# A software pipeline over the heads of a delta rule, and a reordered convolution stage, in a six-layer flow-matching trunk

## What is computed

```
def conv_module(h, w1, b1, dw, dwb, lng, lnb, w2, b2, on_grid):
    a = h @ w1 + b1
    a = a[..., :D_MODEL] * jax.nn.sigmoid(a[..., D_MODEL:])
    a = (dwconv_grid(a, dw) if on_grid else dwconv_seq(a, dw)) + dwb
    a = jax.nn.silu(layer_norm(a, lng, lnb))
    return a @ w2 + b2

def delta_rule_chunked(q, k, v, log_a, beta, s0):
    ...
    a_mat = beta[..., :, None] * jnp.einsum("bhnid,bhnjd->bhnij", k, k) * dec_strict
    rhs = jnp.concatenate([beta[..., None] * v, (beta * jnp.exp(g))[..., None] * k], -1)
    sol = lax.linalg.triangular_solve(eye + a_mat, rhs, left_side=True, lower=True, unit_diagonal=True)
    u_t, w_t = sol[..., :dv], sol[..., dv:]
    p_mat = jnp.einsum("bhnid,bhnjd->bhnij", q, k) * dec_incl
    ...
    def step(s, inp):
        u = ut - jnp.einsum("bhck,bhkv->bhcv", wt, s)
        o = jnp.einsum("bhck,bhkv->bhcv", qt, s) + jnp.einsum("bhij,bhjv->bhiv", pt, u)
        s = gt[..., None, None] * s + jnp.einsum("bhck,bhcv->bhkv", kt, u)
        return s, o
```

## Time and profile before

| what | value |
| --- | --- |
| median of 3 runs | 1915.3 us (1914.95 to 1916.79) |
| the profiled execution, its own time | 1915.8 us |
| its span | 1914.0 us |
| PE busy | 1820.6 us (95%) |
| DVE, ACT, POOL busy | 997.1, 815.5, 266.5 us |
| mean granted TensorE clock | 0.984 of full speed |
| P of head 0 to the last output product of head 7 | 1360.4 to 1541.9 us |
| conv taps on PE | 435.8 to 486.4 us |

### The profile page before, as it was taken

How to read it: one execution, slowest core, us unless ns; L and a number is a source line. 1 busy time by engine, 2 the same in 40 slices (tenths; PEclk the granted TensorE clock), 3 DMA queues, 4 the chain that set the end, 5 groups by cost and what they waited for, 6 DMA issues and landing times.

```text
span 1914.0 us, 30887 instructions
## 1 busy us (share of the span) xinstructions
PE 1820.6 (95%) x11265; PEld 1677.1 (88%) x11265; DVE 997.1 (52%) x1684; ACT 815.5 (43%) x1334; POOL 266.5 (14%) x317
## 2 busy tenths in 40 slices
PE   5999999998999999999999999899899999999998
PEld 3899999688679999988999998878788867999997
DVE  3433444898473434455344448756555547444444
ACT  1333332777553444235444326454444435444322
POOL 2000000476420000010000003000222222000001
PEclk8999999999999999999999999999899989999999
DMA  9774344763566344456444445422000034444440
GB/s 325 219 220 126 117 137 148 255 231 88 186 202 205 112 131 122 134 174 186 131 131 117 134 145 147 131 56 67 9 11 11 11 102 121 127 118 128 133 129 35
DMA packets 369963, 254.16 MB, mean 133 GB/s; under 512 B 9715, under 2 KB 350307, under 8 KB 369891
## 3 DMA queue, kind: packets, MB, share of 16 engines
q1 hardware_dynamic: 369104, 252.89, 43.5%
q10 hardware_dynamic: 787, 0.32, 0.1%
HBM read 250.55 MB, written 2.62 MB: 132 GB/s over the span
## 4 chain that ended last, share of the span: by engine, by line
PE 83%; DVE 8%; issue 3%; DMA 2%; ACT 2%; SPq 1%; DVEq 0%; POOL 0%; ACTq 0%
PE bank L1512 23%; PE bank L1514 23%; PE bank L1513 23%; PE bank L1575 3%; DMA mod_raw<-in_w_mod 2%; PE bank L1940 1%; SPq L470 1%; PE bank L1783 1%; DVE w_lo L997 1%; PE bank L1539 1%; PE bank L1934 1%; PE bank L1751 1%; PE bank L1760 1%; PE bank L1627 1%; PE bank L1798 1%
## 5 line engine op out<-in xcount | busy, mean ns | idle before, releaser
L1512 PE MATMUL bank<-h_hi,w_hi 128*128 128x384 f32 x1920 | 655.5, 341 | 5.3 <-POOL h_lo L599 3.0
L1514 PE MATMUL bank<-h_hi,w_lo 128*128 128x384 f32 x1920 | 644.9, 336 | 0.0
L1513 PE MATMUL bank<-h_lo,w_hi 128*128 128x384 f32 x1920 | 644.6, 336 | 0.0
L997 DVE TENSOR_TENSOR w_lo<-w_raw,w_hi 128x1024 fp32r<-128x1024 f32 x336 | 434.3, 1314 | 190.6 <-ACT w_hi L724 188.3
L724 ACT ACTIVATE w_hi<-w_raw 128x1024 fp32r<-128x1024 f32 x336 | 344.4, 1050 | 313.4 <-PE bank L1514 294.4
L1512 PEld LDWEIGHTS bank<-h_hi,w_hi 128*128 128x128 f32 x1920 | 362.2, 189 | 39.3 <-issue 29.8
L1513 PEld LDWEIGHTS bank<-h_lo,w_hi 128*128 128x128 f32 x1920 | 362.4, 189 | 0.1
L1514 PEld LDWEIGHTS bank<-h_hi,w_lo 128*128 128x128 f32 x1920 | 362.1, 189 | 0.0
L1513 PE MATMUL bank<-act_lo,w_hi 128*128 128x384 f32 x704 | 236.1, 335 | 0.0
L1514 PE MATMUL bank<-act_hi,w_lo 128*128 128x384 f32 x704 | 236.0, 335 | 0.0
L1512 PE MATMUL bank<-act_hi,w_hi 128*128 128x384 f32 x704 | 236.0, 335 | 0.0
(11 more groups left out here) (307 smaller groups left out, 1795.1 us busy)
## 6 DMA issues: line engine op xcount, KB each, us to landing
w_raw<-in_ffn_w_in SPq DMA_DIRECT2D x176, 512.0 KB, 4.7
mod_raw<-in_w_mod SPq DMA_DIRECT2D x132, 512.0 KB, 5.3
w_raw<-in_ffn_w_out SPq DMA_DIRECT2D x64, 448.0 KB, 3.8
w_raw<-in_ffn_w_out SPq DMA_DIRECT2D x32, 512.0 KB, 4.0
w_raw<-in_dn_w_in SPq DMA_DIRECT2D x32, 512.0 KB, 4.0
w_raw<-in_cv_w SPq DMA_DIRECT2D x24, 512.0 KB, 4.3
mod_early<-in_w_mod SPq DMA_DIRECT2D x12, 512.0 KB, 10.0
w_raw<-in_dn_w_out SPq DMA_DIRECT2D x8, 512.0 KB, 4.1
```

Source lines behind the costliest of these rows:

```text
L997: dve.tensor_tensor(w_lo[:, slot], w_raw[:, slot], w_hi[:, slot].bitcast(F32), ALU.subtract).then_inc(w_lo_ready, 1)
L1512: pe.matmul(ps, w_hi[:, w_slot, k], a_hi, start=start, stop=False)
L1513: pe.matmul(ps, w_hi[:, w_slot, k], a_lo, start=False, stop=False)
L1514: return pe.matmul(ps, w_lo[:, w_slot, k], a_hi, start=False, stop=stop)
```

## The change

**Heads.** The loops go over pairs of heads with the buffers that must last doubled (`inv`, `inv_t`, scores, q_decay, k_head; the second set lies in the place of h_hi and h_lo, which are free there), and the last two heads stand behind the loop. Norm spreads, row spreads, scalings, gate differences, exponentials and k·k of head h + 1 are done inside head h, one after the other through bank 7; DVE makes the next head's matrix at the end of head h. Only q·k stays at the start of a head, ahead of P, in bank 7 too.
**Beta.** The system is solved with beta on the columns in place of the rows; so beta isn't spread any more (two of four row spreads go), POOL doesn't multiply v (one copy of the first tile is left, `v_first`), the matrix takes one DVE instruction per tile and direction, and ACT's copy of u has beta as its scale.
**Conv.** ACT makes a row product behind each diagonal, not behind each second; `store_taps` stands 18 diagonals later; PE turns the groups ahead of tap 31, not of tap 8. DVE's list is unchanged there.

```diff
@@ PE, heads
-                with pe.Fori(0, H) as h:
-                    pe.wait_ge(qk_ready, 2 * h + 2)
-                    pe.wait_ge(head_done, h + 1)
-                    for ps, m in ((bank[6], k_head), (bank[7], q_head)):
...
+                def spread_k_norm(n):
+                    pe.wait_ge(sel_ready, n + 1)
+                    spread(bank[7], sel_qk[:, 1], qk_rnorm_hi[:, :], qk_rnorm_lo[:, :]).then_inc(norm_spread, 1)
+                def spread_q_norm(n):
+                    pe.wait_ge(qk_ready, 2 * n + 1)
...
+                def spread_row(n, d):
+                    if d == 0:
+                        pe.wait_ge(qk_ready, 2 * n + 2)
+                    else:
+                        pe.wait_ge(q_exp_ready, 2 * n + 1)
+                    spread(bank[7], sel_row[:, d], rows_hi[:, :], rows_lo[:, :]).then_inc(rows_spread, 1)
...
+                def k_products(n, q):
+                    pe.wait_ge(q_exp_ready, 2 * n + 2)
+                    gram_of(k_heads[q], k_heads[q], kk_ready)
+                def head(h, p, more):
...
+                        if m == 0:
+                            pe.wait_ge(a_step, 2 * h + 2)
+                            gram_of(k_of, q_head, qk_product)
...
+                        if m == 1 and more:
+                            spread_q_norm(h + 1)
...
+                        if m == 0 and more:
+                            pe.wait_ge(scored, 2 * h + 2)
+                            spread_k_norm(h + 1)
...
+                        if m == 1 and more:
+                            spread_row(h + 1, 0)
...
                     solve(0, t_joined, (h + 1) * (2 * UPPER) - 1)
+                    if more:
+                        spread_row(h + 1, 1)
                     solve(1, x_set, 4 * h + 1)
...
-                    pe.wait_ge(sel_ready, h + 2)
-                    spread_norms()
+                    if more:
+                        k_products(h + 1, 1 - p)
+                    solve(2, x_set, 4 * h + 3)
@@ ACT, heads: exponentials(h + 1, 1 - p, 0) behind the levels, and
+                            act.activation(u_sb[:, k % 2, d], u_bank(k, d)[:, 0:P], ACT.Copy,
+                                           scale=beta[:, SCAN[d][k], ds(h + d * H, 1)]).then_inc(u_copied, 1)
                         if k == 1:
+                            if more:
+                                exponentials(h + 1, 1 - p, 1)
                             act.wait_ge(state_in, 16 * h + 16)
                             for d in range(2):
                                 act.wait_ge(s_added, 4 * h + d + 1)
                                 act.activation(s_out[:, d], bank[4 + d][:, 0:P], ACT.Copy).then_inc(s_stored, 1)
@@ DVE, heads
+                def matrix(n, q):
+                    dve.wait_ge(kk_ready, n + 1)
+                    for d in range(2):
+                        dve.wait_ge(decay_ready, 2 * n + d + 1)
+                        for t in range(NT):
+                            last = dve.scalar_tensor_tensor(decay[:, d, t], scores[q][:, d, t], minus_beta[:, t, ds(n + d * H, 1)],
+                                                            bank[7][:, t * P:(t + 1) * P], ALU.mult, ALU.mult)
+                        last.then_inc(a_step, 1)
@@ ACT, conv
+        STORE_LATER = DIAGS + 6
                         diagonal(n)
-                        if n % 2 and left:
+                        if left:
                             row_product(*left.pop(0))
                         for o in (PE_CHUNK, *PE_SEQ):
-                            if n == taps_used(o) + DIAGS - 12:
+                            if n == taps_used(o) + STORE_LATER:
                                 store_taps(o)
@@ PE, conv
                     for n, (o, tap) in enumerate(PE_TAPS):
-                        if n == 8:
+                        if n == TAPS:
                             turn_groups(mod_glu)
```

More of the change, by code:

```diff
@@ L849, in delta_on_scalar @@
                     act.activation(o_all[:, ds(h, 1)], bank[6][:, 0:T].unsqueeze(1), ACT.Copy).then_inc(head_done, 1)
+                for d in range(2):
+                    exponentials(0, 0, d)
+                with act.Fori(0, H // 2 - 1) as i:
+                    for p in range(2):
+                        head(2 * i + p, p, True)
+                for p in range(2):
+                    head(H - 2 + p, p, p == 0)
                 act.wait_ge(head_done, H + 1)
@@ L1335, in delta_on_vector, with head @@
+                        last.then_inc(a_step, 1)
+                def head(h, p, more, select_next):
+                    dve.wait_ge(qk_product, h + 1)
+                    for d in range(2):
+                        dve.tensor_tensor(scores[p][:, d], scores[p][:, d], tiles(bank[7]), ALU.mult).then_inc(scored, 1)
                     for n in range(BASE_LEVEL, LEVELS):
@@ L1364, in delta_on_vector @@
                                                          bank[4 + d][:, 0:P], ALU.mult, ALU.add).then_inc(s_updated, 1)
+                    if more:
+                        matrix(h + 1, 1 - p)
+                scale_k(0, 0)
+                scale_q(0)
+                for d in range(2):
+                    differences(0, 0, d)
+                select(1, 0)
+                matrix(0, 0)
+                with dve.Fori(0, H // 2 - 1) as i:
+                    for p in range(2):
+                        head(2 * i + p, p, True, True)
+                for p in range(2):
+                    head(H - 2 + p, p, p == 0, False)
                 dve.wait_ge(head_done, H + 1)
@@ new lines, in gram_of, with head @@
+                def gram_of(first, second, done):
+                    for t in range(NT):
+                        mm = pe.matmul(bank[7][:, t * P:(t + 1) * P], first[:, t * P:(t + 1) * P], second[:, t * P:(t + 1) * P], start=True, stop=True)
+                    mm.then_inc(done, 1)
+                def k_products(n, q):
+                    pe.wait_ge(q_exp_ready, 2 * n + 2)
+                    gram_of(k_heads[q], k_heads[q], kk_ready)
+                def head(h, p, more):
+                    k_of, inv_of, inv_t_of = k_heads[p], invs[p], invs_t[p]
```

198 lines of the change are left out of this document (102 added, 96 removed).

## The result

| | before | changed |
|---|---|---|
| median, us | 1915.3 (1914.21 to 1917.98, 5 runs) | **1906.1** (1903.84 to 1908.79, 5 runs) |
| ratio, 95% interval | 1 | **0.9948** (0.9935 to 0.9961) |
| profiled execution, its time | 1915.8 | 1908.8 |
| its span | 1914.0 | 1907.0 |
| mean granted clock | 0.984 | 0.984 |

The change makes the kernel faster by 0.52%, 9.2 us in the medians. The forecast was 1896, 19 us faster, with a range of 1888 to 1907: the sign was right and the time lies inside the range, near its upper end, but only half of the gain came; that the time is inside is owed to the width of the range. The profiled execution after is itself 2.7 us above its median, so by place I compare its span with that of before, 7.0 us less; between kernels the medians decide.

The account below looks back on a forecast made before the run. PE was taken to bound the kernel (83% of its chain of waits). Start of heads +6.1, seven periods -19.9, last head -1.0 and conv -4.9 sum to -19.7 us: 1896 by the median, range 1888 to 1907.

Parts of the forecast that it names:

- The start of the heads: Head 0's preparation runs one step after another through bank 7 at the lower clock: 13.5 us before P, +6.1.
- The conv stage: Earlier PE taps, then limited by supply of sums and diagonals: through at 481.4 instead of 486.4, -4.9 us.
- The waits foreseen in a head: Back part of a head: PE waits 1.0 us for ACT's state copy and 0.3 for DVE's matrix.
- the period: P to P of steady heads falls from 23.07 to 20.2 us, -2.84 per head, seven times: -19.9.
- a pair of spread passes is 0.35 us: Price on PE of each norm or row spread pair inserted among a head's other products.
- front part: P to k times state in a steady head: from 10.63 to 11.5 us, +0.9, for three inserted spread pairs.
- back part: k times state to next P in a steady head: from 12.44 to 8.70 us, -3.74.
- The walk of the combination: Conv stage with all three edits: last row product near 466, PE at tap 93 near 472.0, through at 481.4.
- the second case: Heads: serial chain through bank 7 longer than walked, 1.2 us per head, +8.4: 1904; interval 1902 to 1909, chance 0.16.
- the third case: Conv stage: DVE, slowed beside POOL's sums, ends near 487 and the conv gain is nil: 1901, chance 0.14.
- The fourth case: Heads' back part: next head's preparation not hidden, kernel slower from a period over 23.6; fully exposed 1943; chance 0.03.
- The fifth case: Heads: PE bound throughout, without stalls, period near 18.6 us: 1885, chance 0.05.

Follow-up runs that it names:

- E6: Changed kernel with one more spread pair for the next head's k norm, set by itself ahead of T of the first level: 1910.4 us, one execution.
- E5: Changed kernel with each in-loop and starting spread pair made twice, one right behind the other: 1920.2 us, one execution.
- E12: E11 with groups turned ahead of tap 31, stores 18 diagonals later as changed, and row products behind every second diagonal as before the change: 1891.95 us (0.9872).
- E9: Changed kernel with the groups turned ahead of tap 22 in place of tap 31: 1907.9 us, one execution.
- E10: Changed kernel with E3's and E4's edits, the old rhythm of row products and stores, and the groups turned ahead of tap 22: 1894.1 us (0.9879).
- E11: E10 with both row spreads of the next head side by side between P and T of the last level: 1893.5 us (0.9876).
- E3: Changed kernel with ACT copying the state ahead of the next head's second pair of exponentials: 1899.9 us (0.9920).
- E4: Changed kernel with head 0's spreads in four banks and its norm spreads ahead of the wait for ACT's copies: 1900.0 us (0.9919).

## Why the prediction came out as it did

**Right.** The sign, and which places move. The start of the heads: +6.1 forecast, +6.5 measured; P of head 0 13.5 behind the first spread, measured 13.7. The last head: -1.0 and -1.1. The conv stage: PE through at 481.4, measured 481.6; DVE's stall 7.4, measured 7.39; its end 480.8, measured 480.2. The waits foreseen in a head are there, at ACT's state copy (0.8 us, from the start of the second update in the steady head, 3.83, less 2.36 in the last head and 0.69 for the pair; 1.0 forecast) and, just, at the matrix.

**Wrong: the period.** Forecast 20.2, measured 21.82, outside the 19.5 to 21 that I had named as the bounds of a right one. Seven times 2.84 was forecast, the trace shows 8.5 in all, and 11.4 of the 12.7 us by which the sum (-19.7) missed the span (-7.0) are here. The step is the sentence "a pair of spread passes is 0.35 us". I had that from the distance of passes within a group (0.175) and paid it for pairs that stand alone. A pair alone is 0.70 in the front part (2.11 for three, last head against steady head), 0.69 in the back (k times state to outputs 2.14 against 1.45), 0.74 in E6; and 0.35 only behind another pair, E5. The front was thereby 1.1 us too short, three times 0.35. Of the back part's 0.54, the pair's 0.35 comes first; but there the next step waited for ACT, so of that only 0.26 reached the second update (3.83 in place of 3.57), and 0.3 is in the steps behind. Some of it is ACT's copy of u, whose scale from memory I had put at nothing, "at most 0.1 per head": a copy lasts 0.37 us with it and 0.28 before, and the last one stands in PE's way. The clue stood in the trace before, in head 4:

```profile
1471.94 0.49 PE L1796 MATMUL bank<-square,s_new 128*128 128x128 f32 x2
...
1473.03 0.44 PE L1717 MATMUL bank<-rows_hi,sel_row 32*128 32x384 f32 x1
...
1474.62 0.94 PE L1740 MATMUL bank<-k_head 128*128 128x128 f32 x6
```

The four norm passes from 1471.03 take 0.91 until the next product starts, the eight row passes 1.59: 2.50 and not the 2.1 of twelve times 0.175. Each of the two groups pays 0.2 for its borders, whatever its length; cut into four groups of two, that is paid four times.

**Not seen: the parts of the conv stage.** The walk of the combination holds: last row product forecast near 466, measured 466.07; PE behind its first stretch of taps 472.0, measured 472.25. But I let the denser rows and later stores stand as one package that the earlier PE needs. E12 shows that PE can be fed at its full pace without the denser rows, and that these cost 2.2 of the 6 to 7 us that the other two bring. I had walked only the combination that the change has.

**The rivals.** The time fell into the interval of the second case, but not by its mechanism: the handoffs through bank 7 hold PE up in the loop no more than walked; it is PE's own price that was wrong. DVE ended the conv stage by 0.4 to 0.7 us only, not by 6; the collision that the third case names is real and costs through ACT's diagonals (E9, E10). The fourth case has a slip in its arithmetic: with +0.2 from the other places the kernel is slower from a period of 23.04 on; at 23.6 it is slower by 4 us. The fifth case, 18.6, was not reached by any run; the lowest period is 20.88 (E11, E12).

**What the change left lying.** E3's new wait was in my walk, at 1.0 us, and I took it as given; one exchange of two blocks of ACT's code takes it away. The start's +6.1 too was foreseen, and E4 avoids it with banks that are free there.

## What to carry to other kernels

Price an operation by its neighbours: where PE goes over from one kind of product to another, count from the start of the group to the start of what follows it, not the distance of two passes inside, and keep such short foreign groups together. A loop pipelined through one buffer needs its own prologue, since what hides the handoffs in the loop is missing there. When a change is a package, walk each part alone: this one gained 9 us although one of its parts cost 2, the order of two blocks on ACT about 5, and the prologue 6.5.

## What the runs showed of the hardware

- Within a group of spread passes a weight load starts 0.17 us ahead of its product and is hidden; at the group's borders both start together. A pair of spread passes costs 0.35 behind its like and 0.70 to 0.74 alone. Why the border costs this stays open.
- DVE and POOL slow one another, and either can be the loser: 18 column steps 10.35 against 4.81 us; one sum 4.14 us beside steps of DVE that kept their 0.34, against 0.73 alone (E10 and the changed kernel).
- Taking a stall of 6 us from DVE made PE's taps end later by 0.8 (E9) to 1.7 us (E10), and the last mean by 0.7 to 0.8.
- An ACT copy of 128x128 from a bank lasts 0.37 us with its scale from memory and 0.28 without; back to back they start no farther apart for it (0.26 to 0.30 us, before 0.26 to 0.36).
